# Attention by pairs of heads in a two-block fp32 forward pass: two heads' scores and values issued in turn, two sets of score buffers, projections one unit later

## What is computed

```python
q = (h @ w_q + b_q).astype(f32) * (B_DH ** -0.5)
...
s = jnp.einsum('bqkgd,bskd->bkgqs', qb, kk) + bias
s = jnp.where(valid, s, -jnp.inf)
m = jnp.maximum(jnp.max(s, axis=-1), sink)
p = jnp.exp(s - m[..., None])
denom = jnp.sum(p, axis=-1) + jnp.exp(sink - m)
o = jnp.einsum('bkgqs,bskd->bqkgd', p, vv)
return o / jnp.transpose(denom, (0, 3, 1, 2))[..., None]
```

## Time and profile before

| | |
|---|---|
| median of 3 runs | 2077.88 us (2075.93 to 2080.92) |
| the profiled execution, its own time | 2080.16 us |
| its span, first to last instruction | 2078.4 us |
| PE, PEld, DVE, ACT, POOL busy | 95%, 79%, 60%, 37%, 14% of the span |
| mean granted TensorE clock | 0.977 |
| the attention stage, from the first block of query unit 1 to the first block of output unit 2 | 1531.45 to 1664.12 us, 132.7 us |

### The profile page before, as it was taken

The page is one execution under the profiler, slowest core; times in us unless marked ns, Lnnn a source line. Parts: engine busy times, 40 slices in busy tenths (PEclk is TensorE's granted clock), DMA queues, the critical chain, the costliest instruction groups (busy, mean ns, idle before and its releaser), DMA issues.

```text
span 2078.4 us, 27266 instructions
## 1 busy us (share of the span) xinstructions
PE 1978.4 (95%) x9454; PEld 1635.4 (79%) x9454; DVE 1257.3 (60%) x1826; ACT 765.8 (37%) x1350; POOL 284.3 (14%) x215
## 2 busy tenths in 40 slices
PE   6999889999998899999989999999989999999997
PEld 5878677888887688888877788888778787888886
DVE  5886545333335777777754765747658647657475
ACT  4233344233233433343323432424535434324242
POOL 2433123011012100000001100100100011001011
PEclk9999989999998999999999999999999999999998
DMA  4322332332322111111103232332311032323322
GB/s 171 96 79 90 98 104 71 102 102 91 101 91 91 36 46 56 45 46 55 45 11 102 71 112 83 99 102 91 113 50 41 31 102 82 111 83 100 96 97 81
DMA packets 46922, 170.10 MB, mean 82 GB/s; under 512 B 5344, under 2 KB 5504, under 8 KB 46720
## 3 DMA queue, kind: packets, MB, share of 16 engines
q1 hardware_dynamic: 45648, 165.12, 24.7%
q10 hardware_dynamic: 1200, 3.95, 0.5%
HBM read 166.94 MB, written 2.11 MB: 81 GB/s over the span
## 4 chain that ended last, share of the span: by engine, by line
PE 75%; DVE 8%; issue 2%; ACT 2%; POOL 0%; DVEq 0%; ACTq 0%; POOLq 0%
PE ps L246 16%; PE ps L247 16%; PE ps L248 16%; PE ps L258 5%; PE ps L260 5%; PE ps L259 5%; PE ps L581 2%; PE ps L1095 1%; PE ps L1120 1%; PE ps L600 1%; DVE w_lo L226 1%; PE ps L585 1%; DVE scr L1037 1%; PE ps L1106 1%; DVE A_lo L362 1%
## 5 line engine op out<-in xcount | busy, mean ns | idle before, releaser
L226 DVE TENSOR_TENSOR w_lo<-w_raw,w_hi 128x1024 fp32r<-128x1024 f32 x293 | 395.7, 1352 | 196.2 <-ACT w_hi L221 195.9
L221 ACT ACTIVATE w_hi<-w_raw 128x1024 fp32r<-128x1024 f32 x304 | 317.2, 1049 | 233.3 <-PE ps L248 169.5
L246 PE MATMUL ps<-A_hi,w_hi 128*128 128x512 f32 x964 | 376.6, 391 | 10.6 <-DVE scr L885 5.0
L248 PE MATMUL ps<-A_hi,w_lo 128*128 128x512 f32 x964 | 376.0, 390 | 0.0
L247 PE MATMUL ps<-A_lo,w_hi 128*128 128x512 f32 x964 | 376.0, 390 | 0.0
L246 PE MATMUL ps<-B_hi,w_hi 128*128 128x512 f32 x748 | 293.4, 392 | 4.9 <-DVE scr L885 2.2
L247 PE MATMUL ps<-B_lo,w_hi 128*128 128x512 f32 x748 | 292.5, 391 | 0.0
L248 PE MATMUL ps<-B_hi,w_lo 128*128 128x512 f32 x748 | 292.3, 391 | 0.0
L258 PE MATMUL ps<-A_hi,w_hi 128*128 128x512 f32 x460 | 201.4, 438 | 27.4 <-DVE w_lo L226 12.8
L246 PEld LDWEIGHTS ps<-A_hi,w_hi 128*128 128x128 f32 x964 | 181.6, 188 | 50.5 <-issue 12.8
L248 PEld LDWEIGHTS ps<-A_hi,w_lo 128*128 128x128 f32 x964 | 181.5, 188 | 37.9
(11 more groups left out here) (253 smaller groups left out, 2664.3 us busy)
## 6 DMA issues: line engine op xcount, KB each, us to landing
w_raw<-d_ws SPq DMA_DIRECT2D x304, 512.0 KB, 3.5
X<-d_xT SPq DMA_DIRECT2D x4, 512.0 KB, 7.5
X<-d_xT ACTq DMA_DIRECT2D x1, 2048.0 KB, 8.3
d_out<-X SPq DMA_DIRECT2D x4, 512.0 KB, 2.7
scr<-gc_rows ACTq DMA_DIRECT2D x7, 256.0 KB, 3.1
cst<-d_cst SPq DMA_DIRECT2D x1, 800.0 KB, 11.5
par<-d_par SPq DMA_DIRECT2D x1, 344.5 KB, 2.9
scr<-d_pw SPq DMA_DIRECT2D x1, 256.0 KB, 11.6
```

What stands on the lines that cost most here:

```text
L221: nc.scalar.activation(w_hi[:, c], raw[:, c], ACT.Copy).then_inc(S(f"w_hi{s}"), 1)
L226: nc.vector.tensor_tensor(w_lo[:, c], raw[:, c], w_hi[:, c].bitcast(F32), ALU.subtract)\
L246: pe.matmul(ps[bank][:], w_hi[:, c], hi, start=k == 0, stop=False)
L248: last = pe.matmul(ps[bank][:], w_lo[:, c], hi, start=False, stop=k == n - 1)
```

## The change

Six things change together.

1. Scores are issued for both heads of a tile: `scores_pe(t, n)` does key blocks 2n and 2n+1, each matmul of head 0 followed by that of head 1 (rows 0-63 and 64-127 of the array, banks ps2 and ps3, one bank for each head instead of one for each half).
2. Values likewise: `values_pe(t)` does both heads, matmul by matmul, into the two 64-row halves of one bank.
3. `SC` and `PT` get a second set, which lies in `Y`, so tile t+1 can be scored while tile t is still read. `MX` grows from 64 to 96 columns.
4. Projections: iteration t of PE does the whole unit t+2 in pieces of 2, 3 and 3 blocks; unit 1 is done whole before the loop.
5. PE's order for one tile: scores n=0 of t+1, two blocks, scores n=1 of t+1, transposes of head 0, three blocks, transposes of head 1, three blocks, values of both.
6. DVE and ACT are reordered to match.

```diff
+        SC = [[carve(2 * T) for _ in range(2)], [Y[:, 2 * e * T:2 * (e + 1) * T] for e in range(2)]]
+        PT = [[carve(2 * T) for _ in range(2)], [Y[:, 2 * (2 + e) * T:2 * (3 + e) * T] for e in range(2)]]
...
+        def scores_pe(pe, t, n):
+            if n == 0:
+                pe.wait_ge(S("q_t"), count("q_t", t + 1))
+            if t or n:
+                pe.wait_ge(S("s_sc"), count("s_sc", 4 * t + 2 * n))
+            for b in (2 * n, 2 * n + 1):
                 lo = max(b - 1, 0) * P
+                size = P if b == 0 else 2 * P
+                for e in range(2):
+                    out = ps[2 + e][:, (b % 2) * 256 + 256 - size:(b % 2) * 256 + 256]
+                    last = pe.matmul(out, half_rows(QT[t % 2], e)[:, b * P:(b + 1) * P],
+                                     half_rows(KA[t % 2], e)[:, lo:lo + size], start=True, stop=True)
+            last.then_inc(S("s_p"), 1)
...
+        def values_pe(pe, t):
+            if t > 1:
                 pe.wait_ge(S("t_lo"), count("t_lo", t - 1))
+            for n in range(2):
+                pe.wait_ge(S("s_pt"), count("s_pt", 4 * t + 3 + n))
+                for b in (2 * n, 2 * n + 1):
+                    for half_ in range(0 if b else 1, 2):
+                        col = b * 256 + half_ * P
+                        for e in range(2):
+                            key = (b - 1 + half_) * P + 64 * e
+                            last = pe.matmul(ps[6 + t % 2][64 * e:64 * e + 64, b * P:(b + 1) * P],
+                                             VA_T[t % 2][:, key:key + 64], PT[t % 2][e][:, col:col + P],
+                                             start=half_ == 0 or b == 0, stop=half_ == 1)
+            last.then_inc(S("s_o"), 1)
...
-            part(1, 0, KT // 2)
+            part(1, 0, 2)
             pe.wait_ge(S("v_t"), count("v_t", 2))
-            scores_pe(pe, 0)
-            for j in range(2 * KT):
-                t, e = j // 2, j % 2
-                if j < 2 * KT - 1:
-                    scores_pe(pe, j + 1)
-                transpose_pe(pe, j)
-                if e == 0:
-                    part(t + 1, KT // 2, KT)
-                else:
-                    part(t + 2, 0, KT // 2)
-                values_pe(pe, j)
+            scores_pe(pe, 0, 0)
+            part(1, 2, 5)
+            scores_pe(pe, 0, 1)
+            part(1, 5, KT)
+            for t in range(KT):
+                if t < KT - 1:
+                    scores_pe(pe, t + 1, 0)
+                part(t + 2, 0, 2)
+                if t < KT - 1:
+                    scores_pe(pe, t + 1, 1)
+                transpose_pe(pe, t, 0)
+                part(t + 2, 2, 5)
+                transpose_pe(pe, t, 1)
+                part(t + 2, 5, KT)
+                values_pe(pe, t)
...
+            for e in range(2):
+                exps(0, e)
+            for t in range(KT):
+                ahead(act, split_hi, rnd(U_Q, t // SLOTS), t % SLOTS)
+                by_keys(t, 0)
+                if t < KT - 1:
+                    exps(t + 1, 0)
+                by_keys(t, 1)
+                if t < KT - 1:
+                    exps(t + 1, 1)
+                act.wait_ge(S("s_o"), count("s_o", t + 1))
+                a.activation(tile(pairA[0], t), ps[6 + t % 2][:], ACT.Copy).then_inc(S("t_hi"), 1)
...
             q_tile(0)
+            scored(0, 0)
+            scored(0, 1)
+            maxima(0, 0)
+            maxima(0, 1)
+            q_tile(1)
+            normalise(0, 0)
+            normalise(0, 1)
+            for t in range(KT):
+                more = t < KT - 1
+                if more:
+                    scored(t + 1, 0)
+                ahead(dve, split_lo, rnd(U_Q, t // SLOTS), t % SLOTS)
+                if more:
+                    scored(t + 1, 1)
+                    maxima(t + 1, 0)
+                    maxima(t + 1, 1)
+                if t:
                     output_lo(t - 1)
+                if more:
+                    normalise(t + 1, 0)
+                    if t + 2 < KT:
+                        q_tile(t + 2)
+                    normalise(t + 1, 1)
```

More of the change, by code:

```diff
@@ L1072, in build, with sc3 @@
         AW = carve(T)
-        SC = [carve(2 * T) for _ in range(2)]
-        PT = [carve(2 * T) for _ in range(2)]
-        MX = carve(64)
+        SC = [[carve(2 * T) for _ in range(2)], [Y[:, 2 * e * T:2 * (e + 1) * T] for e in range(2)]]
+        PT = [[carve(2 * T) for _ in range(2)], [Y[:, 2 * (2 + e) * T:2 * (3 + e) * T] for e in range(2)]]
+        MX = carve(96)
         DD = carve(T)
-        def sc3(e):
-            return SC[e].rearrange("p (b s) -> p b s", b=NCH)
+        def sc3(t, e):
+            return SC[t % 2][e].rearrange("p (b s) -> p b s", b=NCH)
@@ L1080, in half_rows, with mx_cols @@
+        def mx_cols(t, e, n):
+            first = 24 * (2 * (t % 2) + e) + 4 * n
+            return MX[:, first:first + 4]
+        M_SUM, M_SINK, M_NEG, M_MAX, M_DEN, M_INV = range(6)
         def half_rows(ap, e):
             return ap[64 * e:64 * e + 64, :]
-        def scores_pe(pe, j):
-            t, e = j // 2, j % 2
[L1088 to L1091, removed]
-                lo = max(b - 1, 0) * P
[L1093 to L1098, removed]
@@ new lines, in values_pe @@
+        def values_pe(pe, t):
+            if t > 1:
+                pe.wait_ge(S("t_lo"), count("t_lo", t - 1))
+            for n in range(2):
+                pe.wait_ge(S("s_pt"), count("s_pt", 4 * t + 3 + n))
+                for b in (2 * n, 2 * n + 1):
+                    for half_ in range(0 if b else 1, 2):
+                        col = b * 256 + half_ * P
+                        for e in range(2):
[4 more added lines that the diff above has]
+            last.then_inc(S("s_o"), 1)
@@ L1146, in part @@
                         last.then_inc(S(f"unit_done{s}"), 1)
-                elif first == 0:
-                    unit_wait(pe, rnd(U_BO, 0), s)
-                    part_blocks(pe, s, s, pairA, 0, KT - 2, wait=wait_o)
+                else:
+                    if first == 0:
+                        unit_wait(pe, rnd(U_BO, 0), s)
+                    if first < KT - 2:
+                        part_blocks(pe, s, s, pairA, first, min(end, KT - 2), wait=wait_o)
             unit_after_opening(pe, rnd(U_Q, 0), 0, pairB)
@@ L1191, in exps, with by_keys @@
                     .then_inc(S("s_e"), 1)
                 for b in range(NCH):
-                    sc = SC[e][:, b * 256 + (0 if b else P):(b + 1) * 256]
+                    sc = SC[t % 2][e][:, b * 256 + (0 if b else P):(b + 1) * 256]
                     a.activation(sc, sc, ACT.Exp, bias=neg[:, b:b + 1], accum_out=den[:, b:b + 1])\
                         .then_inc(S("s_e"), 1)
[L1196 to L1200, removed]
+            def by_keys(t, e):
+                if t > 1:
+                    act.wait_ge(S("s_o"), count("s_o", t - 1))
@@ L1224, in attention_dve @@
             for e in range(2):
-                v.memset(SC[e][:, 0:P], -FAR).then_inc(S("zeros"), 1)
+                for p in range(2):
+                    v.memset(SC[p][e][:, 0:P], -FAR).then_inc(S("zeros"), 1)
                 v.tensor_copy(DD[:, e * 256:(e + 1) * 256], cst[:, C_DIST:C_DIST + 256]).then_inc(S("zeros"), 1)
-            dve.wait_ge(S("zeros"), count("zeros", 9))
+            dve.wait_ge(S("zeros"), count("zeros", 11))
             dve.wait_ge(S("kv_R"), count("kv_R", 1))
```

100 lines of the change are left out of this document (33 added, 67 removed).

## The result

| | before | with the change |
|---|---|---|
| median | 2077.88 us (7 runs) | 2083.75 us (7 runs, 2082.84 to 2087.76) |
| ratio | | 1.003, 95% interval 1.0019 to 1.0041 |
| span of the profiled execution | 2078.4 us | 2081.9 us |
| attention stage, first block of query unit 1 to first block of output unit 2 | 132.7 us | 141.7 us |
| mean granted clock | 0.977 | 0.973 |

What follows compares the result with a forecast made beforehand. PE was taken to bound the kernel before; with the change, a chain through three engines. Stage 14.8 + 6 x 15.05 + 27.9 = 133.0 against 132.7, with slow clock +20.5 us: 2098.4 us; 80% range 2076 to 2118.

Steps and rivals of the forecast that it cites:

- full overlap of the pairs: Scores and values of two heads on opposite array halves run simultaneously, 2.6 us off PE's tile; about two in three.
- The faster rival: `split_lo` done before PE reaches the two blocks; turn about 12.6 us, -19 us, 2059 us; chance 0.06.
- start to the first bias-add of the loop: Start of the attention stage, from 1531.45 to the first loop turn: 14.8 us.
- six turns, at full clock: Attention loop, one turn a tile, up to the bias-add of tile 7: 6 x 15.05 us.
- slow clock in the six turns: Two blocks and scores n=1 at half speed behind each 3.4 us gap: 6 x 2.4 us more.
- end, at full clock: End of the attention stage, from the bias-add of tile 7 through the last blocks: 27.9 us.
- slow clock in the end: Half speed behind two gaps at the end of the stage: 5.8 us more.
- the clock's price: Half speed charged behind PE's gaps: 2.4 us in each of six turns and 5.8 us at the end.
- the first gap: End of stage, PE's wait before tile 7's scores n=1: cold clock 2.4 us; the second, before unit 9, 3.4 us.
- the prediction's own sign of being wrong: Tiles 14 us apart or less, L226 done before PE asks, or full clock behind 3 us of idle.
- the chain of ten steps: One loop turn through PE, DVE and ACT, bias-add n=0 to normalising head 1: 15.05 us a tile.
- 2.6 us off PE's 14.06: PE's own work a tile, shortened by paired scores and values under full overlap: 2.6 us less.

Runs made afterwards that it cites:

- split: The changed kernel with ACT and DVE preparing the projection weights one unit further ahead (three instead of two), PE's order kept: 2052.16 us, ratio 0.9877.
- peorder: The changed kernel with only PE's order edited, transposes of head 0 and scores n=1 ahead of the two blocks: 2053.56 us, ratio 0.9888.
- warm: The changed kernel with thirteen extra matmuls, results unread, in PE's gap before the first two blocks: 2074.86 us, ratio to before 0.9981.
- serial: The changed kernel with pairs taken apart: head 0 before head 1 within each half of the scores and over all values: 2088.77 us, ratio 1.0045.

## Why the prediction was right and wrong

**Right.** That it would be slower, and the mechanism, step by step: `split_lo` behind the bias-add, the two blocks behind `split_lo`, scores n=1 behind the blocks; PE idle before L258 in every turn (3.4 us forecast; 4.64 in the first turn, then 2.85 to 3.08); the low clock behind it in each turn, if not at once in each; full overlap of the pairs; the start of the loop 14.8 us in (14.4). The faster rival's mechanism, that the whole lies in whether `split_lo` is done before PE asks for it, was shown by `split` (the split earlier) and `peorder` (PE asks later).

**Wrong: the size.** The stage was forecast at 153.2 us and took 141.7. By terms:

| term | forecast | measured | difference |
|---|---|---|---|
| start to the first bias-add of the loop | 14.8 | 14.43 | -0.4 |
| six turns, at full clock | 6 x 15.05 | 6 x 14.52 (`warm`) | -3.2 |
| slow clock in the six turns | 6 x 2.4 | 6 x 1.96 | -2.6 |
| end, at full clock | 27.9 | 27.1 (worked out below) | -0.8 |
| slow clock in the end | 5.8 | 1.3 | -4.5 |

The step that failed is the clock's price: the prediction charged each gap with half speed for all that PE did until scores n=1, 2.4 us a turn, and "Cold clock here adds 2.4 at the first gap and 3.4 at the second". Together that is 20.2 us; the runs showed 13.1. In the turns it was 2.2 in four and 1.4 and 1.5 in two, against the 14.52 at full clock. At the end it was 1.3 at the first gap, where the clock rose again before scores n=1 (n=1 came 6.39 us after n=0; 7.32 in a turn slow throughout, 5.11 in `warm`), and nothing at the second, of 3.19 us, where it never fell. The end at full clock is put together from two runs, as `warm` too had a slow stretch there: up to the start of unit 9 15.84 us in `warm`, and from there 11.29 in the change, so 27.1. From unit 9 on `warm` took 12.88, so there a gap of the same 3.19 us cost 1.6. Why it cost nothing in the change no run shows. The prediction expected each gap to drop the clock, from two gaps above 3 us (3.06 and 3.29 in the earlier trace rows); with the gap at 1577.93 and the one at 1658.90 there are two behind which it did not fall at once. Full clock behind 3 us of idle was the prediction's own sign of being wrong.

The second step that was off is the chain of ten steps, 0.5 us too long: from the second bias-add to the next first one 9.4 us instead of 9.8, as ACT's copies and exponentials run back to back, and 0.1 ahead of it. A third slip cost nothing: the prediction took 3.05 us for the scores of two heads without overlap, where the earlier trace rows give 2 x 1.72 = 3.44, so its 2.6 us off PE's 14.06 should have been 3.1 (PE is busy 11.15 us a turn in `split`).

**Left open.** The stage is 9.0 us longer (9.0 to 10.6 over two executions of each), the medians differ by 5.9 and 5.1. The other 3 to 5 us lie in code that did not change. Over the executions above, 1526.7 to 1533.5 us pass ahead of the stage and 411.7 to 414.3 behind it. Whether this is chance or follows from the other phase in which the later stages begin was not tested. So of the 14.6 us between forecast and median 11.5 are the stage's and 3.1 are these.

The rule on PSUM that the prediction cited (the Trainium skill, "TensorEngine Tiling (Array Packing)", PSUM Bottleneck) says that the emptying of PSUM may become the bound. With the wait, no engine was the bound. Without it the trace agrees in part: DVE is busy 14.79 of 16 us and PE waits for it twice a turn, 0.3 us each, but of DVE's 10.97 us a turn only some 3.9 (bias-adds 1.13 and 1.41, `A_lo` 0.69, `q_tile` 0.68) are instructions that read PSUM.

## What to carry to other kernels

When an order written by hand puts a producer's step behind a consumer's first result and the consumer's next step behind the producer's, the engines wait for each other in a ring, and all busy shares fall together. Before a faster inner step is put in, look at every wait that moves with it, and at what is queued behind the waiting instruction; one step issued earlier, or one independent step put between, was worth 30 us here, and the overlap that it lets through was worth nothing without it. An idle stretch of TensorE of some 3 us can cost more than itself, here 2.0 us a turn on top: price the work behind it at both clock levels, and do not assume that the clock falls each time.

## What the runs showed of the hardware that was not expected

- Two fp32 matmuls on opposite 64-row halves or 64-column halves ran at the same time: 8 score records in 0.86 us to the next start against 4 in 0.84, 28 value records in 1.75 against 14 in 1.74. It did not take strict alternation: four records of one head before four of the other overlapped as well, while fourteen before fourteen took 2.89, less than twice 1.74 but far from 1.75.
- The clock sometimes fell behind a short gap only after work had resumed: in `serial` the blocks after gaps of 2.43 us start at full speed (0.47), and yet the scores behind them take 2.09 at 1584.14, against 1.13 or 1.14 at full clock. Behind the same gap at 1598.66 it did not fall at all.
- Matmuls that nobody needs, put into the gap, made the kernel 8.9 us faster.
